# Moving activations at other byte distances from the weights in the state buffer

## What is computed

```
first_block:   h += mix(rmsnorm(h))          # mLSTM heads and a gated convolution, merged, then w_out
               h += ffn(rmsnorm(h))          # w_up (2048 x 11008), causal conv of 3 taps, silu*val, w_down
               h  = rmsnorm(h)
second_block:  x += rmsnorm(gla_mixer(rmsnorm(x)))   # gated linear attention, 4 heads
               x += rmsnorm(mla_mixer(rmsnorm(x)))   # latent attention, 16 heads
```

## Time and profile before

| | us |
|---|---|
| median of three runs | 2237.8 |
| the profiled execution | 2238.66 |
| its span, first to last instruction | 2236.9 |
| TensorE busy with matmuls | 2148.0 (96%) |
| VectorE busy | 1300.0 (58%) |
| ScalarE busy | 1188.9 (53%) |
| share of the 16 DMA engines, weight stream | 49.3% |

### The profile page before, as it was taken

The page is one execution under the profiler, slowest core; times in us unless marked ns, Lnnn a source line. Parts: engine busy times, 40 slices in busy tenths (PEclk is TensorE's granted clock), DMA queues, the critical chain, the costliest instruction groups (busy, mean ns, idle before and its releaser), DMA issues.

```text
span 2236.9 us, 46586 instructions
## 1 busy us (share of the span) xinstructions
PE 2148.0 (96%) x17596; PEld 2102.7 (94%) x17596; DVE 1300.0 (58%) x1641; ACT 1188.9 (53%) x1565; POOL 256.2 (11%) x325
## 2 busy tenths in 40 slices
PE   6999999999999999999999999999999978999996
PEld 5999999999999999999999999989999978899996
DVE  5655664444456666666666555556655466765544
ACT  5444445545456566565665454644554445565643
POOL 2000000001110000000001111000100124111212
PEclk7999999999999999999999999999999999999998
DMA  4454545555555455555546556445444443444453
GB/s 149 171 176 179 173 164 189 190 199 179 188 200 189 173 184 178 179 178 178 186 170 224 207 207 225 171 170 188 169 169 169 169 150 131 172 150 150 150 176 124
DMA packets 54927, 393.83 MB, mean 176 GB/s; under 512 B 6097, under 2 KB 6225, under 8 KB 7522
## 3 DMA queue, kind: packets, MB, share of 16 engines
q1 hardware_dynamic: 54432, 392.19, 49.3%
q10 hardware_dynamic: 450, 1.02, 0.1%
HBM read 391.09 MB, written 2.10 MB: 176 GB/s over the span
## 4 chain that ended last, share of the span: by engine, by line
PE 60%; issue 19%; DVE 10%; ACT 7%; POOL 3%; DVEq 1%; ACTq 1%; DMA 0%; POOLq 0%
PE acc L554 17%; PE acc L556 17%; PE acc L555 17%; ACT w_hi L921 4%; DVE w_lo L1326 3%; PE tok L596 2%; PE tok L597 2%; PE tok L598 2%; DVE f_pre L1551 2%; ACT L1097 1%; DVE f_val L1562 1%; DVE f_val L1558 1%; DVE f_act L1571 1%; POOL sumsq_g L1894 1%; PE att L614 1%
## 5 line engine op out<-in xcount | busy, mean ns | idle before, releaser
L1326 DVE TENSOR_TENSOR w_lo<-raw,w_hi 128x1024 fp32r<-128x1024 f32 x740 | 903.9, 1236 | 792.2 <-ACT w_hi L921 790.1
L554 PE MATMUL acc<-n_hi,w_hi 128*128 128x256 f32 x3488 | 988.7, 283 | 37.0 <-POOL n_lo L1903 19.0
L555 PE MATMUL acc<-n_lo,w_hi 128*128 128x256 f32 x3488 | 979.9, 281 | 0.0
L556 PE MATMUL acc<-n_hi,w_lo 128*128 128x256 f32 x3488 | 979.7, 281 | 0.0
L921 ACT ACTIVATE w_hi<-raw 128x1024 fp32r<-128x1024 f32 x740 | 760.4, 1053 | 385.7 <-DMA raw<-stream_in 169.5
L554 PEld LDWEIGHTS acc<-n_hi,w_hi 128*128 128x128 f32 x3488 | 661.4, 190 | 43.7 <-issue 20.4
L555 PEld LDWEIGHTS acc<-n_lo,w_hi 128*128 128x128 f32 x3488 | 661.5, 190 | 0.5
L556 PEld LDWEIGHTS acc<-n_hi,w_lo 128*128 128x128 f32 x3488 | 661.1, 190 | 0.0
L554 PE MATMUL acc<-f_hi,w_hi 128*128 128x256 f32 x688 | 189.9, 276 | 0.0
L555 PE MATMUL acc<-f_lo,w_hi 128*128 128x256 f32 x688 | 189.9, 276 | 0.0
L556 PE MATMUL acc<-f_hi,w_lo 128*128 128x256 f32 x688 | 189.9, 276 | 0.0
(11 more groups left out here) (313 smaller groups left out, 2975.4 us busy)
## 6 DMA issues: line engine op xcount, KB each, us to landing
raw<-stream_in SPq DMA_DIRECT2D x370, 1024.0 KB, 4.8
x<-x_in SPq DMA_DIRECT2D x4, 512.0 KB, 7.3
out<-x SPq DMA_DIRECT2D x4, 512.0 KB, 2.7
v_bias<-v_bias_in ACTq DMA_DIRECT2D x1, 512.0 KB, 8.7
par<-params_in ACTq DMA_DIRECT2D x1, 287.0 KB, 5.3
pos_i<-positions_in ACTq DMA_DIRECT2D x1, 128.0 KB, 6.7
gk<-gk_in ACTq DMA_DIRECT2D x1, 68.0 KB
```

Of the source, the lines that this page charges most:

```text
L554: nc.tensor.matmul(out, w_hi[:, s, wc], hi[:, k, :], start=first, stop=False)
L555: nc.tensor.matmul(out, w_hi[:, s, wc], lo[:, k, :], start=False, stop=False)
L556: return nc.tensor.matmul(out, w_lo[:, s, wc], hi[:, k, :], start=False, stop=last)
L1326: nc.vector.tensor_tensor(w_lo[:, s, :], raw[:, s, :], w_hi[:, s, :].bitcast(fp32), ALU.subtract).then_inc(lo_ready, 1)
```

## The change

Only addresses change. No instruction is added, taken away or moved, on any engine. The distance of the start of the activations from the start of the weights, modulo 256 bytes, becomes:

| tensor | before | after |
|---|---|---|
| `n_hi`, `n_lo` | 32, 32 | 192, 192 |
| `yc_hi`, `yc_lo` | 192, 192 | 224, 224 |
| `hm_hi`, `hm_lo` | 192, 192 | 160, 160 |
| `mg_hi`, `mg_lo` | 192, 192 | 160, 160 |
| `f_hi`, `f_lo` | 192, 192 | 192, 128 |
| `og_hi`, `og_lo` | 192, 192 | 192, 64 |
| `mo`, `c` (high and low) | 192, 192 | 192, 192 |

The tensors that are placed behind these move along by up to 480 bytes.

```diff
-LINE = 128
+LINE = 256
...
-        apart = sb("apart", [P, 8])
+        apart = sb("apart", [P, LINE // 4 * 3 // 4])
...
-        arena_start = -(-(nc.sbuf_base - LINE // 2) // LINE) * LINE + LINE // 2
+        arena_start = -(-(nc.sbuf_base - LINE // 4) // LINE) * LINE + LINE // 4
...
-            def place(self, name, shape, dt=fp32):
+            def place(self, name, shape, dt=fp32, skip=0):
+                self.at += skip
...
-        yc_hi = a.place("yc_hi", [P, C_TILES, T], fp32r)
+        yc_hi = a.place("yc_hi", [P, C_TILES, T], fp32r, skip=32)
...
-        hm_hi = a.place("hm_hi", [P, C_TILES, T], fp32r)
+        hm_hi = a.place("hm_hi", [P, C_TILES, T], fp32r, skip=192)
...
-        f_lo = a.place("f_lo", [P, F_TILES, T], fp32r)
+        f_lo = a.place("f_lo", [P, F_TILES, T], fp32r, skip=192)
...
-        og_lo = a.place("og_lo", [P, KT, T], fp32r)
+        og_lo = a.place("og_lo", [P, KT, T], fp32r, skip=128)
```

## The result

The changed kernel takes 2256.9 us (median of 4 runs, 2254.1 to 2260.4) against 2238.3 for the kernel before (4 runs, 2237.7 to 2240.7). The ratio is 1.0081, its 95% interval 1.0067 to 1.0094. It is 0.8% slower, where 0.9% faster was forecast.

The account below looks back on a forecast made before the run. TensorE, busy 96% of the span, was taken as the bound. Savings of 25.4 us on `n` less 6.0 us for the other distances took 19.4 off the median 2237.8, giving 2218.4 us, 0.9% faster; range 2211 to 2229.5.

Parts of the forecast that it names:

- The step that failed: All matmuls on `n`: at 192 they would take 113.3 ns, 3.5 to 4.5 ns less than at 32.
- What `n` gives back: Savings from moving `n` to 192, summed over mix, merge, rank, gla, latent, krope, mla and wup: 25.4 us.
- mix, 7.9: Mix stage: 1920 matmuls on `n` each save 4.1 ns, 7.9 us, since TensorE waits for nobody there.
- merge, 5.5: Merge stage: 1536 matmuls on `n` each save 3.6 ns, 5.5 us.
- rank and gla, 5.3 and 1.8 for the loaded activations: Rank and gla: matmuls moving `n` save 5.3 us; in gla, 384 loading activations as weights at 512 columns save 1.8.
- latent and mla, 1.5 and 2.0: Cheaper matmuls on `n` save 1.5 us in latent and krope, and 2.0 us in mla.
- wup, 0.4: Wup stage: only 0.4 us saved, because the chain there runs through ScalarE and VectorE and TensorE would idle more.
- the rival in which it follows TensorE: Wup shortens with TensorE after all, another 16.5 us, total 2201.9 us; chance 0.04.
- `yc`, `hm`, `mg`: Merge and wout: 1536 matmuls at 224 or 160 turn as dear as `n`, costing 6.0 us, upper bound 9.4.
- `f_lo`, `og_lo`: Low halves at 128 and 64 stay on multiples of 64: cost 0, upper bounds 3.7 or 11.0 us.
- "Slower": Price of `n` goes with its program place, so nothing is gained; moved arena tiles cost 6.0, 2243.8 us; chance 0.07.
- "Placement has no effect at all": Whole kernel: addresses do not matter to TensorE, time stays 2237.8 us; chance 0.05.

Follow-up runs that it names:

- kernels with two and three at 32: Everything at 192, plus two or three spare matmuls on zeros at distance 32 ahead of some 30 stretches: 2226.5 us with two, 2227.0 with three.

## Why the prediction was wrong

**The step that failed** is "The change puts `n` at 192, where `f`, `mg` and `mo` are measured. That is the safest step of this forecast." The measurement was good, three stages at 113.3 ns, and the conclusion that 113.3 is the price of the distance was not. Distance 192 has two prices. `f` had the lower one because it stood right behind matmuls at 32, and `mg` because merge, which runs into it, began so; `mo` had it too, with other matmuls in between. The change takes away what had put `f` there. And the price of `n` was an average of two as well: the earlier trace rows were read as one step of 117.2 to 117.8 ns, 4.1 above the fast one, where the tensor has 116.7 ns in some stretches and 117.8 in others, and those at 117.8 gave nothing back. (The 117.3 ns read in gla is 116.7 without the late start that its 469 ns show.) That is one error, one price for one address, and it hit on two sides.

**What `n` gives back: 25.4 us forecast, 4.7 measured** (2.4 at the start and mix, 4.8 in rank and gla, less 1.5 in merge, 0.1 in latent and 0.9 in mla, where `c` counts too).
- mix, 7.9 and 1.0: in each head the stretches up to tile 16 came down from 116.7 to 113.4, and the long one from tile 16 on stayed at 117.8.
- merge, 5.5: the opposite sign. `n` is slow throughout, 117.8 where it was 116.7 before, 1440 x 1.06 = 1.5 us of loss. With `hm` and `yc` at 192 the same `n` did give 5.2 us, nearly what was forecast (250.2 against 255.4, in eight kernels).
- rank and gla, 5.3 and 1.8 for the loaded activations: 4.8 of 7.1. In each head the stretch from tile 18 on was slow, as it had been before. The loaded ones did as forecast at 512 columns: 388 ns long in the list for 395 before, a step of 228.9 ns against 233.3. They too have two steps at 192: it is 233.4 in gla with everything at 192. At 256 columns it is 117.8 against 118.4, so 0.6 ns each and not 2.6; the value between two far bounds lay nearer to no gain. (The first mix head of the kernels with two and three at 32 has 113.4 there.) The 119.4 of the prediction came from a row with a break in it, seen by its longest matmul of 387 ns.
- latent and mla, 1.5 and 2.0: nothing. In latent `n` is at 117.4 for 117.2. In mla it came down, from 116.9 to 115.3 on average, some 1.3 us, but `c`, whose distance of 192 stays, went from 113.5 to 117.6, some 2.0 us, and its 96 matmuls of 512 columns from 228.8 to 233.4 ns.
- wup, 0.4: right, with its reason. In each of the fifteen kernels, before and after among them, it is 499.1 to 500.4 us long, with `n` at 32, 64, 128, 192 or 448. ScalarE and VectorE set it, as the earlier trace rows said; the rival in which it follows TensorE is out.

**What the other distances cost: 6.0 us forecast, 25.7 measured.**
- `yc`, `hm`, `mg`: the place was right and the size short, some 5.2 ns and not 3.9, 3.7 us in merge (where `hm` had averaged 114.0 before) and 4.1 in wout. It lies within the bound of 9.4.
- `f_lo`, `og_lo`: cost taken 0, with 11.0 us as the upper bound "if all three of a triple do". wdown is 11.1 and glaout 3.4 us longer, 14.5 together, which is over the bound too: it counted 3.9 ns a matmul, and they are 5.4 ns dearer on `f` and 4.4 on `og`. (For `og` this may be nothing but the slow step of 192, also 117.8.) That they stay on multiples of 64 was the reason, and multiples of 64 are no class: 64 costs 117.8 nearly everywhere and 128 118.7. wdown growing was one of the prediction's own signs that it is wrong. (Four of the five kernels with `n` at 192 or 448, `f` wholly at 192 and no spare matmuls at 32 had `f` at 117.8, so some 9.2 of the 11.1 us would probably have been lost anyway.)
- `mo`, not in the sum since its distance stays: 3.4 us, the slow step at an unchanged distance.

The two terms together are off by 20.7 + 19.7 = 40.4 us, which is what parts the profiled execution, 2259.65, from the 2219.3 forecast for it.

**The rivals.** "Slower" had the right sign, and the balance turned where it said, `n` giving back less than a quarter (4.7 of 25.4 us); the step that it names, over 116.6 ns, was not met on average (115.8). Its mechanism ("goes with where it is in the program") is half of the truth; the address sets which steps there are, and the place in the program, what ran just before, which of them is taken. Its reason against, that `n` differs in nothing else that TensorE sees, overlooked this. "Placement has no effect at all" is out: four kernels that differ in addresses alone, everything at 192, at 448, at 64 and at 128, take 2240.6, 2239.0, 2264.7 and 2277.6 us. That is also where the rule of the Trainium skill (page "SBUF — State Buffer", section "Who interferes with whom") does not carry as far as the prediction took it: TensorE's step changes with the address of the activations, although its instructions and those of the other engines are the same. The rule speaks of engines that wait for each other; what TensorE's own two reads do to each other no run here shows. No stretch of such matmuls of 256 columns had a mean step below 113.3 ns at any distance, so the 109.2 ns estimated from the Trainium skill, page "TensorE: Matmul & The Clock Gate", section "Back-to-back issue gap", stays unreached here; the page gives that formula for an isolated matmul, and these are a stream with a load of weights for each.

**What stays open.** What is shown is that each of the distances 32, 64, 128 and 192 has two steps, that a stretch keeps its own, that matmuls at 32 (two or more, at the full clock) set the fast one for what follows at 192 without a break, and that three at 192 do not. Not shown are what 160 and 224 hand on, which step a break leaves outside mix and gla (`og`, behind a wait and a stretch at half clock, was fast at both 192 and 448 and slow at both), and why a single product with `h_sum` or `o_sum` turns the step where it does. The mechanism behind it all, and so the reason why a distance has the steps it has, is open, and so is whether it is the distance: a kernel with the weights moved and the activations left would tell. Only `token_tiles` has the roles exchanged: the moving weights stay, and the step of 512 columns still goes with the place of the loaded activations (233.3 with `n` at 32; 228.9 or 233.4 at 192). The kernels at 192 vary more from run to run (the one with `n` at 192 and the arena at 448 from 2228.9 to 2246.6 us); that would fit breaks in wup and mla that come out differently, but one run of each was traced.

## What to carry to other kernels

A step that is measured at one place belongs to the place and to what runs ahead of it until it has been seen both ways. Before a price is put on an address, look for the same tensor at two prices within one profile, and ask what stood before each. A mean between two clean values is a sign of a mixture. In this kernel, where matmuls run back to back for milliseconds, the place of the activations modulo 256 bytes, with the weights fixed, is worth 1.7% between the best and the worst (2238.8 and 2277.6 us), and 2.3% with two spare matmuls at 32 behind the breaks, the best found; 160, 224, 128 and 64 were dearer here, for either half.

## What the runs showed of the hardware

Steps of fp32r matmuls, 128x128 by 256 columns with a load of the weights for each, at the full clock (granted 0.99 to 1.00). The weights start at 128 modulo 256 in all of them:

| distance modulo 256, high and low half | ns | what follows it at 192 without a break |
|---|---|---|
| 32 | 116.7 or 117.8 | the fast step, behind either |
| 64 | 117.8, in a few stretches 113.3 | not run |
| 128 | 118.7, in a few stretches 120.0 | not run |
| 160 | 118.6 to 118.8 | the slow step, seen only where it was slow ahead of 160 too |
| 224 | 118.6 | the same |
| 192 | 113.3 or 117.8 | the one it has |
| 192 and 128 | 118.7 to 118.9 | both seen |
| 192 and 64 | 117.8 | not seen |

The 2064 matmuls on `f` keep one step to the last, and a step is passed from tensor to tensor where no break lies between. That a stream of equal instructions has two steady speeds at 192, 3.9% apart, at the same clock and the same addresses, that two matmuls on another tensor move it from one to the other, and that a single product between two stretches parted a fast from a slow one in 48 places of 48, was not expected.
